# Encoder layer with recurrence and mixture of experts: other roles of the recurrence's buffers, tiles at jobs 3, 6, 10 and 13, preparation of all eight blocks ahead of attention

## The reference

```python
h = rmsnorm(x, norm1_g);  proj = h @ w_in            # q 512, k 128, v 128, xr 512, gate 512 columns
q, k = axial_rope(rmsnorm_heads(q)), axial_rope(rmsnorm_heads(k))   # 8 q heads, 2 kv heads of 64
attn_out = softmax(q k^T / 8) v                      # per sequence, 512 x 512 scores per head
xc = centred_conv4(xr)
for each direction: r, i = sigmoid(blockdiag(xc)); a = exp(-8 r softplus(-lam))
                    h = scan(a, sqrt(1 - a*a) * i * xc)      # forward and backward in time
lru_out = (h_fwd + h_bwd) * gelu(gate)
x = x + concat(attn_out, lru_out) @ w_out
y = x + expert_choice_moe(rmsnorm(x, norm2_g))       # 16 experts, 64 tokens each per sequence
```

## Time and profile before

| | us |
|---|---|
| median of 3 runs | 1079.77 (1078.56 to 1084.36) |
| the profiled execution, its time | 1081.51 |
| its span, first to last instruction | 1079.7 |
| TensorE busy | 991.9 (92%) |
| VectorE busy | 813.7 (75%) |
| ScalarE busy | 708.3 (66%) |
| GpSimd busy | 336.0 (31%) |
| job stage | 42.8 to 218.7 |
| attention, scores of the first unit to the last product with v | 218.7 to about 362 |
| output projection, norm, routing | to about 499 |
| experts | to 1079.7 |

### The profile page before, as it was taken

One profiled execution on the slowest core, in us unless ns is written; L12 is line 12 of the kernel. 1 busy time (PEld: TensorE's weight loads), 2 busy tenths in 40 slices (PEclk: granted clock), 3 DMA queues, 4 the chain that ended last, 5 costly groups with the idle time before them and its releaser, 6 DMA issues.

```text
span 1079.7 us, 14786 instructions
## 1 busy us (share of the span) xinstructions
PE 991.9 (92%) x4935; PEld 824.2 (76%) x4935; DVE 813.7 (75%) x1030; ACT 708.3 (66%) x931; POOL 336.0 (31%) x190
## 2 busy tenths in 40 slices
PE   3999999978899999934999999999999999999995
PEld 3789997866766788833788888888888888888874
DVE  5658789867798322263898889988898889888883
ACT  6367767566798211141898777877797778877773
POOL 0000040065366000041064346533663356413320
PEclk9999999999999999966999999999999999999997
DMA  6111101000301543386899999999999999999851
GB/s 247 51 45 45 44 13 40 1 1 1 117 1 61 197 155 118 117 318 233 312 381 387 386 393 399 383 390 393 390 392 383 386 392 403 385 383 373 310 167 28
DMA packets 75232, 248.95 MB, mean 231 GB/s; under 512 B 9356, under 2 KB 16568, under 8 KB 75192
## 3 DMA queue, kind: packets, MB, share of 16 engines
q1 hardware_dynamic: 70584, 231.64, 56.0%
q0 software_dynamic: 4608, 16.78, 6.2%
HBM read 231.63 MB, written 16.78 MB: 230 GB/s over the span
## 4 chain that ended last, share of the span: by engine, by line
PE 77%; DVE 10%; ACT 7%; issue 3%; DMA 1%; SPq 0%; POOL 0%; ACTq 0%; POOLq 0%
PE bank L934 23%; PE bank L936 23%; PE bank L935 23%; PE bank L940 5%; DVE e_lo L1460 2%; ACT e_hi L865 2%; PE bank L1094 1%; PE bank L1057 1%; PE bank L1058 1%; ACT prob L825 1%; DMA x_nat<-in_x_prompt_dram 1%; DVE probT_lo L1398 1%; DVE row_stat L1386 1%; DVE top_idx L1445 1%; ACT probT_hi L818 1%
## 5 line engine op out<-in xcount | busy, mean ns | idle before, releaser
L934 PE MATMUL bank<-e_hi,xsT_hi 128*128 128x512 f32 x512 | 201.7, 394 | 1.6 <-DVE xsT_lo L1465 1.4
L936 PE MATMUL bank<-e_hi,xsT_lo 128*128 128x512 f32 x512 | 199.8, 390 | 0.0
L935 PE MATMUL bank<-e_lo,xsT_hi 128*128 128x512 f32 x512 | 199.8, 390 | 0.0
L639 POOL COPY idx_now<-idx_all 128x1 uint32 (+1 forms) x16 | 157.0, 9811 | 28.1 <-DMA y_dram<-ys,idx_now 28.1
L865 ACT ACTIVATE e_hi<-raw_gate 128x1024 fp32r<-128x1024 f32 x128 | 134.6, 1060 | 35.3 <-PE bank L936 33.8
L1460 DVE TENSOR_TENSOR e_lo<-raw_down,e_hi 128x1024 fp32r<-128x1024 f32 x128 | 146.9, 1220 | 2.4 <-ACT e_hi L865 0.6
L1460 DVE TENSOR_TENSOR e_lo<-raw_up,e_hi 128x1024 fp32r<-128x1024 f32 x128 | 146.7, 1219 | 1.4 <-ACT e_hi L865 1.3
L1460 DVE TENSOR_TENSOR e_lo<-raw_gate,e_hi 128x1024 fp32r<-128x1024 f32 x122 | 141.2, 1219 | 4.6 <-ACT e_hi L865 4.6
L865 ACT ACTIVATE e_hi<-raw_up 128x1024 fp32r<-128x1024 f32 x128 | 126.4, 1055 | 1.7 <-PE bank L936 0.3
L865 ACT ACTIVATE e_hi<-raw_down 128x1024 fp32r<-128x1024 f32 x128 | 125.2, 1060 | 1.1 <-PE bank L936 0.9
L934 PEld LDWEIGHTS bank<-e_hi,xsT_hi 128*128 128x128 f32 x512 | 96.5, 189 | 22.3 <-DVE xsT_lo L1465 1.8
(11 more groups left out here) (217 smaller groups left out, 2086.4 us busy)
## 6 DMA issues: line engine op xcount, KB each, us to landing
raw_gate<-in_exp_w_gate_dram SPq DMA_DIRECT2D x64, 1024.0 KB, 10.7
raw_up<-in_exp_w_up_dram SPq DMA_DIRECT2D x64, 1024.0 KB, 8.3
raw_down<-in_exp_w_down_dram SPq DMA_DIRECT2D x64, 1024.0 KB, 7.1
w_raw<-in_w_in_dram SPq DMA_DIRECT2D x7, 1024.0 KB, 5.2
wo_raw<-in_w_out_dram SPq DMA_DIRECT2D x8, 512.0 KB, 4.3
y_dram<-x SPq DMA_DIRECT2D x8, 512.0 KB, 5.5
h_rows<-h SPq DMA_DIRECT2D x8, 512.0 KB, 3.3
x_nat<-in_x_prompt_dram SPq DMA_DIRECT2D x4, 512.0 KB, 5.9
```

The costliest lines, as they stand in the source:

```text
L639: pool.tensor_copy(idx_now[:, 2:3], idx_all[:, bass.ds(e, 1)] if not isinstance(e, int) else idx_all[:, e:e + 1]).then_inc(idx_copied, 1)
L934: pe.matmul(out, l_hi, r_hi, start=first, stop=False)
L935: pe.matmul(out, l_hi, r_lo, start=False, stop=False)
L936: return pe.matmul(out, l_lo, r_hi, start=False, stop=last)
```

## The change

1. `ib_of(ct, d)` and `mult_of(ct, d)`: from tile to tile the buffers `ib` and `mult` swap roles. The second sigmoid of a tile then waits for `scaled` (the product with the root) of the tile before, in place of its sum; in return `decay` waits for the tile before to be summed. In scan both scalings come ahead of the four scans.
2. Banks of xr are emptied by ScalarE, not by VectorE.
3. Tiles begin at jobs 3, 6, 10, 13 in place of 3, 7, 11, 15.
4. All eight blocks are squared, summed, rotated and scaled in the job stage; the order of these steps is another: sums and rotations of blocks 0 and 1 at job 17, of 2 and 3 at job 18 (where rstd follows), norm, hi and lo of blocks 0 to 3 one block after the other at job 19, blocks 4 to 7 at jobs 20 and 21, their norms at 22 and 23, transposes at 25, hi and lo of blocks 4 and 5 at 26. GpSimd's late steps are gone; hi and lo of blocks 6 and 7 stay where they were.
5. `wo_lo` of the first six row groups is made by GpSimd, not by VectorE, in the same slots.

```diff
+    LRU_FROM = (3, 6, 10, 13)
...
+    lru_at(LRU_FROM[0], ("conv", 0))
+    for ct, c in enumerate(LRU_FROM):
+        lru_at(c + 1, ("gates", ct, 0))
+        lru_at(c + 2, ("gates", ct, 1))
+        lru_at(c + 3, ("decay", ct))
+        if ct < CT - 1:
+            lru_at(c + 3, ("conv", ct + 1))
+        lru_at(c + 4, ("scan", ct))
...
+    FIRST_PREP = LRU_FROM[CT - 1] + 4
...
+    lru_at(FIRST_PREP - 1, ("square", 0))
     for b in range(BPS):
...
+        lru_at(FIRST_PREP + b // 2, ("sum", b), *([("square", b + 1)] if b + 1 < BPS else []), ("rotate", b))
+    lru_at(FIRST_PREP + 1, ("rstd", 0))
     for b in range(BPS):
...
+        lru_at(FIRST_PREP + 2, ("norm", b), ("hi", b), ("lo", b))
+    lru_at(FIRST_PREP + 3, ("square", BPS))
     for b in range(BPS, NB):
...
+        lru_at(FIRST_PREP + 3 + (b - BPS) // 2, ("sum", b), *([("square", b + 1)] if b + 1 < NB else []), ("rotate", b))
+    lru_at(FIRST_PREP + 4, ("rstd", 1))
+    for b in range(BPS, NB):
+        lru_at(FIRST_PREP + 5 + (b - BPS) // 2, ("norm", b))
+    lru_at(NG * JOBS - 3, *[(stage, n) for stage in ("transpose", "out") for n in range(BPS)])
     for b in range(BPS, EARLY_BLOCKS):
...
+        lru_at(NG * JOBS - 2, ("hi", b), ("lo", b))
...
         for kind, n in attn:
-            if kind == "late":
-                late_step(*n)
-            elif kind == "split_lo" and n >= 2 * WO_EARLY:
+            if kind == "split_lo" and n < 2 * WO_EARLY:
+                k, cols = n // 2, slice(n % 2 * D // 2, (n % 2 + 1) * D // 2)
+                pool.wait_ge(wo_hi_done, n + 1)
+                pool.tensor_tensor(wo_lo[k][:, cols], wo_raw[k][:, cols], wo_hi[k][:, cols].bitcast(F32), ALU.subtract).then_inc(wo_lo_pool, 1)
+            elif kind == "split_lo":
...
+                elif what == "xr":
+                    act.wait_ge(proj_done, nth + 1)
+                    act.activation(xr_pad[:, c0 + j % 2, j // 2, CONV_LEFT:CONV_LEFT + S], bank[:, nth % 4, :], ACT.Copy).then_inc(xr_out, 1)
...
                 if ct:
-                    act.wait_ge(scan_done, ct)
-                act.activation(ib[d][:, :], bank[:, 6:8, :].rearrange("p a b -> p (a b)"), ACT.Sigmoid,
+                    act.wait_ge(scaled, 2 * (ct - 1) + d + 1)
+                act.activation(ib_of(ct, d)[:, :], bank[:, 6:8, :].rearrange("p a b -> p (a b)"), ACT.Sigmoid,
...
                 act.wait_ge(lru_c_done, 1)
+                if ct:
+                    act.wait_ge(scan_done, ct)
...
                 for d in range(2):
                     dve.wait_ge(root_done, 2 * ct + d + 1)
-                    link(dve.tensor_tensor(ib[d][:, :], ib[d][:, :], mult[d][:, :], ALU.mult))
+                    dve.tensor_tensor(ib_of(ct, d)[:, :], ib_of(ct, d)[:, :], mult_of(ct, d)[:, :], ALU.mult).then_inc(scaled, 1)
+                for d in range(2):
+                    dve.wait_ge(scaled, 2 * ct + d + 1)
+                    x = ib_of(ct, d)
                     for s in range(SEQS):
```

More of the change, by code:

```diff
@@ L115, in layer_program, with ib_of, mult_of @@
     mult = [at(f"mult{d}", R3 + (16 + 16 * d) * K, [P, T], F32) for d in range(2)]
+    def ib_of(ct, d):
+        return (ib, mult)[ct % 2][d]
+    def mult_of(ct, d):
+        return (mult, ib)[ct % 2][d]
     xc_hi = at("xc_hi", SM + 12 * K, [P, T], F32R)
@@ L288, in layer_program, with lru_at @@
     LRU_AT = {}
[L289 to L295, removed]
+    LRU_FROM = (3, 6, 10, 13)
+    def lru_at(n, *steps_in):
+        LRU_AT.setdefault(n, []).extend(steps_in)
@@ L303, in layer_program @@
     for b in range(BPS):
-        prepare_at(PREP_FROM + b // 2, ("square", b))
+        lru_at(FIRST_PREP + b // 2, ("sum", b), *([("square", b + 1)] if b + 1 < BPS else []), ("rotate", b))
+    lru_at(FIRST_PREP + 1, ("rstd", 0))
     for b in range(BPS):
[L306 to L311, removed]
@@ L312, in layer_program @@
-    for b in range(BPS, NB):
[L313 to L316, removed]
+        lru_at(FIRST_PREP + 2, ("norm", b), ("hi", b), ("lo", b))
+    lru_at(FIRST_PREP + 3, ("square", BPS))
+    for b in range(BPS, NB):
+        lru_at(FIRST_PREP + 3 + (b - BPS) // 2, ("sum", b), *([("square", b + 1)] if b + 1 < NB else []), ("rotate", b))
@@ L349, in layer_program @@
     beside = {2: [("v", 0)], 15: [("hi", 6)], 16: [("lo", 6)], 23: [("hi", 7)], 24: [("lo", 7)]}
-    LATE_STEPS = [("swap", 0), ("swap", 1), ("swap", 2), ("cos", 0), ("cos", 1), ("cos", 2), ("add", 0), ("add", 1), ("scale", 0), ("scale", 1)]
-    for i, b in enumerate(range(EARLY_BLOCKS, NB)):
-        for k, part in enumerate(LATE_STEPS):
-            beside.setdefault(3 + 10 * i + k, []).append(("late", (b, part)))
     for n in range(2 * BPS, USES * NB):
@@ L1317, in _ @@
                     dve.tensor_tensor(out, out, gate_now[:, i % 2, :], ALU.mult).then_inc(gated, 1)
-                elif what == "xr":
-                    dve.wait_ge(proj_done, n + 1)
-                    dve.tensor_copy(xr_pad[:, c0 + j % 2, j // 2, CONV_LEFT:CONV_LEFT + S], bank[:, n % 4, :]).then_inc(xr_out, 1)
             elif kind == "conv":
@@ L1350, in _ @@
                     dve.wait_ge(root_done, 2 * ct + d + 1)
[L1351 removed]
+                    dve.tensor_tensor(ib_of(ct, d)[:, :], ib_of(ct, d)[:, :], mult_of(ct, d)[:, :], ALU.mult).then_inc(scaled, 1)
+                for d in range(2):
+                    dve.wait_ge(scaled, 2 * ct + d + 1)
+                    x = ib_of(ct, d)
                     for s in range(SEQS):
[L1353 removed]
+                        a, b = (v[:, s * S:(s + 1) * S] for v in (decay[d], x))
                         if d:
[L1355 removed]
+                            a, b = (v[:, (s + 1) * S - 1:s * S - 1 if s else None:-1] for v in (decay[d], x))
                         ins = dve.tensor_tensor_scan(b, a, b, 0.0, ALU.mult, ALU.add)
                 link(ins)
[L1358 removed]
+                dve.tensor_tensor(lru_out[:, ct, :], ib_of(ct, 0)[:, :], ib_of(ct, 1)[:, :], ALU.add).then_inc(scan_done, 1)
             elif kind in PREPARE:
```

72 lines of the change are left out of this document (12 added, 60 removed).

## The result

The changed kernel takes 1099.93 us (median of 4 runs, 1098.1 to 1100.42) against 1080.49 for the kernel before (4 runs, 1078.56 to 1084.36): 19.4 us slower by the medians. Forecast were 1097.3 us and a range of 1086 to 1105. The profiled execution took 1099.97 us, with a span of 1097.8.

What follows compares the result with a forecast made beforehand. Bound: the order in which VectorE reaches what TensorE waits for, TensorE itself being almost always busy. 18.5 + 1.7 - 0.7 - 2 = +17.5 us; from the median 1079.8, 1097.3 us; range 1086 to 1105.

Steps and rivals of the forecast that it cites:

- Parts 1 and 2: Recurrence: swapped `ib`/`mult` roles remove ScalarE's 3.63 us wait at tile 3; ScalarE empties xr; worth nothing by themselves.
- Part 3: Closer tiles: TensorE waits 2.6 us before tile 1's gates and 2.0 us before tile 3's.
- Part 4: Before job 20: last scan and two blocks precede `w_lo` on VectorE; wait of 8.6 us in place of 2.15.
- part 6: Granted clock: half-rate stretches behind the new waits of TensorE cost +1.7 us.
- Part 5: All eight blocks prepared before attention: job 24 at 210.3, job 25 at 217.4, scores at 237.2, +18.5 us.
- Part 7: Attention's first half: late steps taken off GpSimd give -0.7 us (0 to -3).
- Part 8: Attention's second half: `wo_lo` of six row groups from VectorE to GpSimd gives -2 us (-4 to +7).
- Rival C: Attention's second half: GpSimd becomes the bound, +3 instead of -2, 1102 us; chance 0.05.
- B: Only the first wait counts, as VectorE and ScalarE catch up during jobs 20 to 23: 1089 us; chance 0.13.
- D: Faster: `w_lo` ready before job 19 ends, if last `lru_out` ends by about 161: 1078 or 1073 us; chance 0.08.
- E: No effect: waits of tiles 1 and 3 and a smaller `w_lo` wait repaid in attention, 1077 to 1084; chance 0.06.

Runs made afterwards that it cites:

- experiment 6: Kernel before with only `ib` and `mult` swapping roles, scalings ahead of the scans, and xr banks emptied by ScalarE: 1079.94 us (0.9989).
- experiment 2: Changed kernel with tiles back at jobs 3, 7, 11, 15: 1093.56 us (1.0112 to the kernel before).
- experiment 4: Changed kernel with rotation and scaling of blocks 6 and 7 back on GpSimd in attention: 1099.22 us (1.0159 to the kernel before).
- experiment 5: Kernel before with only `wo_lo` of the first six row groups moved to GpSimd: 1077.09 us (0.9961).
- experiment 3: Changed kernel with first gate group's `w_lo` before job 17's sums, norm/hi/lo two blocks per job, blocks 4 to 7 one per job: 1091.37 us (1.0088 to kernel before).
- experiment 9: Kernel before with `ib`/`mult` roles swapped, xr emptied by ScalarE, first gate group's w at job 17, tile 3 at job 14 not 15: 1087.40 us (1.0058).
- experiment 1: Changed kernel with first gate group's `w_hi` and `w_lo` ahead of sums and rotations of blocks 0 and 1: 1098.08 us (1.0162 to the kernel before).

## Why the prediction was right, step by step

**Parts 1 and 2: nothing.** Right as far as the runs tell: 0.5 us less in experiment 6, with an interval that reaches 1.

**Part 3: waits of 2.6 and 2.0 us.** Measured 2.54 and 1.93, and neither is there with tiles four jobs apart (experiment 2).

**Part 4: a wait of 8.6 us for `w_lo`, ending at 180.3.** Measured 8.39, ending at 182.46. The last `lru_out` was forecast at 170.7 and ended at 172.8; from there each step lies 2.1 us later than forecast, and the distances hold. The 2.1 us are the later start of the stage (43.34 against 42.77: 0.6) and the loss at half clock behind the wait at 84.44 (2.96 us of work in 3.40 at half rate, so 1.5), which the sum had under its part 6.

**Part 5: job 24 at 210.3, job 25 at 217.4, scores 18.1 + 1.7 later.** Measured 212.51, 220.21 and 19.79 later at 240.00; a block of norm, `hi` and `lo` took 2.77 us where 2.78 stood in the sum. The first is the same 2.1 later. For job 25 one step was mis-sized: the sum had a wait of 217.4 - 210.3 - 5.45 = 1.65 us at full clock. In fact TensorE was never early: job 24 ran at half rate until 217.1 and took 220.21 - 212.51 = 7.70 us in place of 5.45, and by its end the gelu it needed (started at 219.02, and 0.6 long) had been done for 0.6 us. So the wait was there only as slower work. That too is why experiment 4 gained nothing: without its steps the gelu comes sooner, but job 24 does not end sooner.

**Part 6: clock, +1.7.** Three stretches, not two: 1.5 us at 84; from 182.46 to 186.40, 3.9 us at half rate, thus 2.0; and from 212.51 to 217.10, 4.6 us, thus 2.3, of which 1.7 cover a wait. The middle one the prediction had put inside waits of VectorE: it was hidden there, for job 24 starts when the gelu is done. So 1.5 + 0.6 = 2.1 us count, against 1.7.

**Part 7: -0.7.** Not settled. Attention's first half is 70.2 us against 69.95 (the row of the kernel before stands in experiment 5):

```profile
240.00:310.22 70.22, 57.94 (x305) 45.57 (x304) 49.49 (x104) 45.33 (x104) 21.94 (x32) 0.90 0.11 39
```

But the granted clock is 0.90 in it and was 0.93, and TensorE is busy 1.3 us longer with as many matmuls, so a gain of the size forecast may lie under the clock. Experiment 4, with the same clock of 0.90, has 0.5 us more with the steps on GpSimd. A gain of 3, the bound, does not fit either.

**Part 8: -2.** The direction was right, the size was not: -3.4, measured alone (experiment 5) and in every kernel that has it (second half of attention 54.2 to 54.3 us, against 57.6 to 57.7 in the others). That was nearer to the bound of -4. The sum had left out that GpSimd's scalings became shorter too; whether the other 1.4 us come from that was not measured. Rival C, GpSimd as the bound, falls: in the changed kernel it is busy 46.0 of 54.25 us (window of attention's second half, the fifth busy time):

```profile
310.22:364.47 54.25, 52.48 (x288) 41.46 (x287) 45.14 (x101) 51.42 (x122) 45.98 (x53) 1.00 0.03 10
```

TensorE is busy 52.5 us of the same window and ScalarE 51.4, so of the stretch there is little left to win by moving more off VectorE.

The rule of the Trainium skill ("Perfetto Trace Analysis", section Optimizing Scalar/DVE Operations) which the prediction weighed, that moving work between VectorE and GpSimd might not help, is not borne out for these 12 subtractions: it would have given zero or a loss.

**The sum.** The profiled executions lie 1099.97 - 1081.51 = 18.5 us apart, where 17.5 were forecast. The job stage lost 20.8 (18.5 + 1.7 forecast), the stage began 0.6 later, attention's first half lost 0.3 (-0.7 forecast) and its second gained 3.4 (2 forecast); the remaining 0.2 lie in the rest of the execution. The other 1.6 us by which the forecast was low are the step from the profiled execution to the median: the kernel before was profiled 1.7 us above its median, the changed one at it. That step is chance, and so is part of the nearness of the sum: against the forecast the stage and its start came 1.2 us worse and attention's first half 1.0, the second half 1.4 better. What was no luck are the places and lengths of the four waits, which make up most of what the job stage lost.

**The rivals.** B had the two engines catching up during jobs 20 to 23. They had the slack for it (in the changed kernel ScalarE is busy 116 us of 197), but each pair of `hi` waited for a norm and each `lo` for the `hi`: 2.77 us per block, idle 1.83 of it on ScalarE. Experiment 3 is B brought about by another order, and only in part. D decided at `lru_out` by 161; it ended 11.8 us after that. E did not come about, and in experiment 9 even one tile moved closer cost something, mostly (4.61 us of TensorE's waits against 1.93) by the preparation that came between its halves.

**What stays open.** Which waits are followed by half clock. The same wait of 2.5 us before tile 1 is followed by such a stretch in the changed kernel and by none in experiments 1, 3 and 4 (the row is that of experiment 1):

```profile
83.40:86.80 3.40, 3.39 (x17) 2.86 (x18) 3.40 (x4) 2.25 (x3) 0.00 (x0) 1.00 0.12 25
```

Likewise the wait of 2.1 us for `w_lo`: followed by it in the kernel before, not in experiment 5, where it was 2.13, nor in experiment 6, where it was 2.46. The wait of 1.93 us before tile 3 has one in experiment 9 and none in the changed kernel. The wait of 2.62 us in experiment 3 has none. The waits of 4 us and more in the job stage all have one. No run here tells the shorter ones apart, so a short wait is priced at its length plus 0 to 1.7 us. Not tried either: all eight blocks prepared ahead of attention, with the tiles four jobs apart and the order of experiment 3; it would show whether early preparation can be had for nothing.

## What to carry to other kernels

When several engines walk one list of steps, look for the instruction that frees TensorE (a bank emptied, a weight split) and ask what stands ahead of it in its own queue and whether any of that waits for the other engine; busy time tells nothing of it, and a step moved "earlier" can put others between the halves of a chain. A wait taken away is worth only what the next such instruction allows, so forecast the following two waits as well. Work moved from an engine in the path to one with slack can also shorten what that engine already had, when the two had lengthened each other (`mixL_lo` from 1454 to 1290 ns). The 9.1 us taken off VectorE were worth 3.4, and they kept that worth beside all the other edits here.

## What the runs showed of the hardware

The granted clock falls to 0.50 (1.2 in place of 2.4 GHz) during a wait of TensorE or soon behind it, and stays there for some time after it has resumed: in the kernel before it fell 1.3 us after the end of a wait of 2.15 us (171.2, 169.88); in the changed kernel it fell at 176.2, 2.1 us into the wait that ended at 182.46, and rose at 186.4; at the next long wait it fell 3.2 us after the wait began and rose 4.6 us after its end. So these two waits cost 2.0 and 2.3 us more than their length, and the part of the stretch inside the wait costs nothing. Over the other runs the same reading gives 1.5 us (the wait of 8.14 us in experiment 1, clock at 0.50 until 201.4) to 2.8 (that of 4.00 us, until 215.1), so the longer wait does not have the longer tail. VectorE's and GpSimd's subtractions lengthen each other when they overlap: GpSimd's 1.29 us became 1.72, VectorE's 0.68 became 0.82. A table load of ScalarE (1.28 us) in front of a gelu was paid again at 217.73 because a root stood between two gelus.
